# Depthwise convolution of a two-block kernel: seven of 31 taps moved to GpSimd, one from TensorE to VectorE's share, a modulation pair placed behind the taps

## The reference

```
u = h @ w_pw1 + b_pw1            # 1024 -> 2048
a, g = split(u);  v = a * sigmoid(g)
v = dwconv(v, w_dw, b_dw)        # depthwise, 31 taps, pad 15, each channel alone
v = silu(layernorm(v, ln_g, ln_b))
return v @ w_pw2 + b_pw2
```

## Time and profile before

| | |
|---|---|
| median of three runs | 2652.66 us |
| the profiled execution | 2652.95 us |
| its span | 2651.1 us |
| PE busy | 2338.6 us, 88% |
| DVE busy | 1311.8 us, 49% |
| ACT busy | 927.6 us, 35% |
| POOL busy | 732.1 us, 28% |
| L1234, the taps on DVE | 448 instructions, 235.9 us |

### The profile page before, as it was taken

How to read it: one execution, slowest core, us unless ns; L and a number is a source line. 1 busy time by engine, 2 the same in 40 slices (tenths; PEclk the granted TensorE clock), 3 DMA queues, 4 the chain that set the end, 5 groups by cost and what they waited for, 6 DMA issues and landing times.

```text
span 2651.1 us, 35320 instructions
## 1 busy us (share of the span) xinstructions
PE 2338.6 (88%) x13455; PEld 1920.8 (72%) x13455; DVE 1311.8 (49%) x2171; ACT 927.6 (35%) x1388; POOL 732.1 (28%) x344
## 2 busy tenths in 40 slices
PE   3888647999999997999979999989967888999998
PEld 3777436888888886767767787767636887778877
DVE  3599973433123324568553213456665554542441
ACT  4211143543123313455444323434452222442341
POOL 2122102223222221310133434433102222344342
PEclk7999868999999998999989999999887998999999
DMA  7656301122112221200023323332100001233332
GB/s 250 223 192 213 108 7 58 48 64 75 52 56 63 69 59 52 72 25 1 18 87 87 97 86 95 104 104 80 52 0 1 1 1 43 85 90 92 95 96 87
DMA packets 337222, 204.70 MB, mean 77 GB/s; under 512 B 5918, under 2 KB 335304, under 8 KB 336968
## 3 DMA queue, kind: packets, MB, share of 16 engines
q1 hardware_dynamic: 331915, 194.02, 24.4%
q10 hardware_dynamic: 5180, 8.94, 1.0%
HBM read 200.74 MB, written 2.20 MB: 77 GB/s over the span
## 4 chain that ended last, share of the span: by engine, by line
PE 38%; issue 31%; DVE 15%; POOL 10%; ACT 3%; DVEq 1%; DMA 1%; ACTq 0%; POOLq 0%
PE ps L575 10%; POOL w_lo L517 10%; PE ps L576 10%; PE ps L577 10%; DVE ps L1234 9%; PE ps L2449 1%; PE ps L2447 1%; PE ps L2439 1%; PE ps L1500 1%; DVE n_t L960 1%; DVE m L2608 1%; PE ps L776 1%; ACT w_hi L547 0%; DVEq L2629 0%; DMA x_rows<-in_ctx 0%
## 5 line engine op out<-in xcount | busy, mean ns | idle before, releaser
L517 POOL TENSOR_TENSOR w_lo<-raw,w_hi 128x1024 fp32r<-128x1024 f32 (+1 forms) x253 | 645.2, 2552 | 1523.0 <-ACT w_hi L547 1504.4
L575 PE MATMUL ps<-x_hi,w_hi 128*128 128x512 f32 (+1 forms) x1864 | 683.1, 366 | 67.8 <-DVE x_lo L1137 49.4
L576 PE MATMUL ps<-x_lo,w_hi 128*128 128x512 f32 (+1 forms) x1864 | 669.0, 359 | 0.0
L577 PE MATMUL ps<-x_hi,w_lo 128*128 128x512 f32 (+1 forms) x1864 | 667.2, 358 | 0.0
L547 ACT ACTIVATE w_hi<-raw 128x1024 fp32r<-128x1024 f32 (+1 forms) x251 | 280.9, 1120 | 836.7 <-PE ps L577 830.8
L575 PEld LDWEIGHTS ps<-x_hi,w_hi 128*128 128x128 f32 x1864 | 356.6, 191 | 141.1 <-issue 68.5
L576 PEld LDWEIGHTS ps<-x_lo,w_hi 128*128 128x128 f32 x1864 | 357.3, 192 | 53.0 <-issue 3.8
L577 PEld LDWEIGHTS ps<-x_hi,w_lo 128*128 128x128 f32 x1864 | 356.7, 191 | 51.8
L1401 DVE SCALAR_TENSOR_TENSOR f_a<-ps,prm,f_a 128x511 f32<-128x511 f32 (+2 forms) x176 | 116.1, 681 | 375.6 <-ACT f_b L1367 364.7
L575 PE MATMUL ps<-g_hi,w_hi 128*128 128x512 f32 (+1 forms) x704 | 259.5, 369 | 14.7 <-DVE g_lo L1410 10.5
L576 PE MATMUL ps<-g_lo,w_hi 128*128 128x512 f32 (+1 forms) x704 | 257.6, 366 | 0.0
(11 more groups left out here) (346 smaller groups left out, 3017.1 us busy)
## 6 DMA issues: line engine op xcount, KB each, us to landing
raw<-in_ffn_w_up SPq DMA_DIRECT2D x88, 512.0 KB, 3.8
ada_tail<-in_ada_w SPq DMA_DIRECT2D x22, 1024.0 KB, 8.2
raw<-in_ffn_w_down SPq DMA_DIRECT2D x32, 704.0 KB, 4.5
raw<-in_w_up SPq DMA_DIRECT2D x44, 512.0 KB, 3.8
ada_s<-in_ada_w SPq DMA_DIRECT2D x20, 1024.0 KB, 9.0
raw<-in_conv_w_pw SPq DMA_DIRECT2D x24, 512.0 KB, 4.1
raw<-in_w_down SPq DMA_DIRECT2D x16, 704.0 KB, 4.6
raw<-in_w_in SPq DMA_DIRECT2D x17, 512.0 KB, 3.9
```

The source lines that it names most:

```text
L517: pool.tensor_tensor(M.w_lo[:, slot, 0:K * P], M.raw[:, slot, 0:K * P], M.w_hi[:, slot, 0:K * P].bitcast(F32), ALU.subtract).then_inc(lo_r ...
L575: pe.matmul(o, wh, hi[:, k, t0:t0 + tn], start=(k == 0), stop=False)
L576: pe.matmul(o, wh, lo[:, k, t0:t0 + tn], start=False, stop=False)
L577: return pe.matmul(o, wl, hi[:, k, t0:t0 + tn], start=False, stop=(k == K - 1))
```

## The change

TensorE's taps go from three to two (`PE_TAPS`), GpSimd takes seven (`POOL_TAPS`), VectorE has the remaining 22 (28 before). For tile j GpSimd (`taps_pool`) multiplies `vp` with the column of weights into an accumulator `pc` (first tap) or into one of two scratch tiles `pt` (the others: two instructions, 512 and 256 columns), waits for its own product, and adds it to `pc` (768 columns). VectorE adds `pc` to the sum in PSUM behind its last tap, when GpSimd's seven are done. `vp` becomes a ring of three tiles; `pc` and `pt` lie where its other tiles lay. In GpSimd's order the block of tile j - 1 stands behind the `w_lo` of chunks 2j and 2j + 1; the additions to `cv_sum` come one tile later than before. The gating product of the next tile stands in front of VectorE's tap number 13 instead of 18. On TensorE, `taps_pe(j)` comes behind the second modulation pair; the third, where there is one, comes behind `taps_pe(j)`.

```
--- before.py
+++ after.py
@@ -16,7 +16,8 @@
 HD = 64
 TAPS = 31
 PAD = TAPS // 2
-PE_TAPS = 3
+PE_TAPS = 2
+POOL_TAPS = 7
 EPS = 1e-6
 GN_EPS = 64e-5
 L2_EPS = 1e-12
@@ -237,7 +238,9 @@
         self.ada_first = [ada_x[:, i, :, :] for i in range(6)] + [ada_tail[:, i, :, :] for i in range(2)]
         self.ada_ring = [ada_tail[:, i, :, :] for i in range(2)] + [ada_s[:, i, :, :] for i in range(2)]
 
-        self.vp = at("vp", r_g, [KD, self.vw])
+        self.vp = at("vp", r_g, [3, self.vw])
+        self.pc = at("pc", r_g + 4 * self.vw * 4, [2, TOK])
+        self.pt = at("pt", r_g + 4 * self.vw * 4 + 2 * TOK * 4, [2, TOK])
         self.cv = at("cv", r_g + KD * self.vw * 4, [KD, TOK])
 
         o = r_g
@@ -402,6 +405,8 @@
     gate_ready = sem("gate_ready")
     v_ready = sem("v_ready")
     tap_done = sem("tap_done")
+    pool_tap = sem("pool_tap")
+    pool_prod = sem("pool_prod")
     cv_ready = sem("cv_ready")
     cv_cent = sem("cv_cent")
     diag_ready = sem("diag_ready")
@@ -825,7 +830,7 @@
         for tap in range(PE_TAPS):
             for t0, t1, at in ((0, SEQ, VLAT), (SEQ, TOK, VCTX)):
                 mm = pe.matmul(M.pair(j % 2, t0, t1), M.diag[j % 2][tap],
-                               M.vp[:, j, at - PAD + tap:at - PAD + tap + t1 - t0], start=(tap == 0),
+                               M.vp[:, j % 3, at - PAD + tap:at - PAD + tap + t1 - t0], start=(tap == 0),
                                stop=(tap == PE_TAPS - 1))
         mm.then_inc(pe_taps, 1)
 
@@ -837,7 +842,7 @@
             ada_products(pe, M.ada_ring[2 * n % 4:2 * n % 4 + 2], ADA_FIRST + 2 * n)
 
         for j in range(8):
-            first, *others = pairs_of(j)
+            first, second, *third = pairs_of(j)
             if j == 0:
                 first_two(pe, "pw1", BOTH, "n10")
                 ada(first)
@@ -845,9 +850,10 @@
                 products(pe, "pw1", j // 2, 2 * (j % 2), BOTH)
                 ada(first)
                 products(pe, "pw1", j // 2, 2 * (j % 2) + 1, BOTH)
-            for n in others:
+            ada(second)
+            taps_pe(pe, j)
+            for n in third:
                 ada(n)
-            taps_pe(pe, j)
         turn_mods_pe(pe, 1)
 
     def add_mods(dve, lo, hi, n):
@@ -1197,8 +1203,8 @@
 
     VLAT, VCTX = PAD, SEQ + 3 * PAD
 
-    DVE_TAPS = TAPS - PE_TAPS
-    NEXT_AT = 18
+    DVE_TAPS = TAPS - PE_TAPS - POOL_TAPS
+    NEXT_AT = 13
 
     def pw1_dve(dve):
         q0 = Q0["pw1"]
@@ -1208,7 +1214,7 @@
             dve.wait_ge(tile_done, done(q0 + 2 * j + 2))
             dve.wait_ge(gate_ready, done(j + 1))
             for t0, t1, at in ((0, SEQ, VLAT), (SEQ, TOK, VCTX)):
-                ins = dve.scalar_tensor_tensor(out=M.vp[:, j, at:at + t1 - t0], in0=M.pair(j % 2, t0, t1),
+                ins = dve.scalar_tensor_tensor(out=M.vp[:, j % 3, at:at + t1 - t0], in0=M.pair(j % 2, t0, t1),
                                                scalar=M.col("conv_b_pw1", j), in1=M.gate[:, j % 2, t0:t1],
                                                op0=ALU.add, op1=ALU.mult)
             ins.then_inc(v_ready, 1)
@@ -1223,16 +1229,40 @@
             for i in range(DVE_TAPS):
                 if i == NEXT_AT and j < 7:
                     gated(j + 1)
-                tap = PE_TAPS + i
+                tap = PE_TAPS + POOL_TAPS + i
                 for n, (t0, t1, at) in enumerate(((0, SEQ, VLAT), (SEQ, TOK, VCTX))):
-                    src = M.vp[:, j, at - PAD + tap:at - PAD + tap + t1 - t0]
+                    src = M.vp[:, j % 3, at - PAD + tap:at - PAD + tap + t1 - t0]
                     w = M.prm[:, cw + tap * 8 + j:cw + tap * 8 + j + 1]
                     o = M.pair(j % 2, t0, t1)
-                    step = 2 * (DVE_TAPS * j + i) + n
+                    step = (2 * DVE_TAPS + 1) * j + 2 * i + n
                     if i:
                         dve.wait_ge(tap_done, done(step - 1))
                     dve.scalar_tensor_tensor(out=o, in0=src, scalar=w, in1=o, op0=ALU.mult, op1=ALU.add)\
                         .then_inc(tap_done, 1)
+            dve.wait_ge(tap_done, done((2 * DVE_TAPS + 1) * (j + 1) - 1))
+            dve.wait_ge(pool_tap, done(POOL_TAPS * (j + 1)))
+            dve.tensor_tensor(M.pair(j % 2), M.pc[:, j % 2, :], M.pair(j % 2), ALU.add).then_inc(tap_done, 1)
+
+    def taps_pool(pool, j):
+
+        acc = M.pc[:, j % 2, :]
+        pool.wait_ge(v_ready, done(j + 1))
+        if j >= 2:
+            pool.wait_ge(tap_done, done((2 * DVE_TAPS + 1) * (j - 1)))
+        for n in range(POOL_TAPS):
+            tap = PE_TAPS + n
+            c = COL["conv_w_dw"] + tap * 8 + j
+            dst = M.pt[:, n % 2, :] if n else acc
+            for t0, t1, at in ((0, SEQ, VLAT), (SEQ, TOK, VCTX)):
+                ins = pool.tensor_scalar(dst[:, t0:t1], M.vp[:, j % 3, at - PAD + tap:at - PAD + tap + t1 - t0],
+                                         M.prm[:, c:c + 1], zero_col, ALU.mult, ALU.add)
+            ins.then_inc(pool_prod, 1)
+            pool.wait_ge(pool_prod, done(POOL_TAPS * j + n + 1))
+            if n:
+                pool.wait_ge(pool_tap, done(POOL_TAPS * j + n))
+                pool.tensor_tensor(acc, acc, dst, ALU.add).then_inc(pool_tap, 1)
+            else:
+                pool.drain().then_inc(pool_tap, 1)
 
     def pw1_act(act):
         groups = 0
@@ -1257,7 +1287,7 @@
 
     def copy_conv(act, j):
         pair = j % 2
-        act.wait_ge(tap_done, done(2 * DVE_TAPS * (j + 1)))
+        act.wait_ge(tap_done, done((2 * DVE_TAPS + 1) * (j + 1)))
         act.activation(M.cv[:, j, :], M.pair(pair), ACT.Identity, bias=M.col("conv_b_dw", j)).then_inc(cv_ready, 1)
         act.wait_ge(cv_ready, done(j + 1))
         act.drain().then_inc(evac, 2)
@@ -1302,7 +1332,11 @@
         for j in range(8):
             diag_pool(pool, j)
             low_stream(pool, "pw1", 2 * j, 2 * j + 2)
-            cv_sum_pool(pool, j - 2)
+            cv_sum_pool(pool, j - 3)
+            if j:
+                taps_pool(pool, j - 1)
+        cv_sum_pool(pool, 5)
+        taps_pool(pool, 7)
         low_stream(pool, "pw2", 0, 2)
         cv_sum_pool(pool, 6)
         low_stream(pool, "pw2", 2, 8)
@@ -2731,7 +2765,7 @@
 
     @block.gpsimd
     def _(pool):
-        prime(pool, [P_S.sem, lo_ready, zero_ready, diag_ready, cv_sum])
+        prime(pool, [P_S.sem, lo_ready, zero_ready, diag_ready, cv_sum, pool_tap, pool_prod])
         pool.memset(M.p_rows[:, PT - 1, :], 0.0)
         pool.memset(M.one[:, 0:1], EPS)
         pool.memset(M.one[:, 1:2], GN_EPS)
```

18 lines of the change are left out of this document (12 added, 6 removed).

## The result

The changed kernel takes 2635.52 us (median of five runs, 2631.04 to 2639.96) against 2652.86 for the kernel before on the same chip: a ratio of 0.9931, 95% interval 0.9914 to 0.9948, or 17 us less. The prediction said 2660, 7 us more. It had most of the structure of the stage right, the price of one instruction wrong, and the end of the stage wrong.

A forecast was written before the change was run, and what follows sets the result against it. VectorE's chain was taken to bound the first convolution's stage; after the change, 273.75 plus three GpSimd blocks of 25.5 put its end at 350.3 against 343.43, +6.9 us on 2652.95, so 2660, range 2640 to 2679.

The forecast's parts named there:

- the price of GpSimd's TENSOR_SCALAR: GpSimd's taps: a 512- and a 256-column product together taken as 2.0 us, giving a block of 25.5 us.
- it can only push up: GpSimd's taps: two operations and two column operands, unpriced by the trace, could only raise the product's cost; no size given.
- The lowest end, 1.05: GpSimd's taps: cheapest bound for the two products, 1.05 us with a small fixed part, giving a block of 18.9.
- if the block is under 21 us: Sign on GpSimd's block of seven taps: under 21 us, the forecast is wrong and rival 3 holds.
- 273.75 + 3B: VectorE's end of the stage, B being GpSimd's block of seven taps; with 25.5 it gives 350.3 against 343.43.
- A second term: the end: Stage's end: after the last gating product VectorE needs 34.55 us for taps and additions, ending at 350.3.
- Gating 7 comes 36.0 + 1.1 later: Last tile's gating product on VectorE: comes 36.0 + 1.1 us behind the end of GpSimd's block 5.
- The start: Stage's start: VectorE begins near 88.8 instead of 101.15, stops from 102.5 to 116.1, and the head start is lost.
- The cycle: Two tiles of the stage: 41.3 us plus GpSimd's block, 66.8 with 25.5, where they took 60.9 before.
- rival 1: GpSimd's product pair costs like a two-input operation, 2.30 us; GpSimd bounds throughout; +16 us, 2669; chance 0.21.
- rival 3: GpSimd's products have a small fixed part, pair 1.05 us, block 18.9; -13 us, 2640; chance 0.21.
- The shares: Chances given for the whole kernel's outcome: faster 0.27, same 0.27, slower 0.46.

The follow-up runs named there:

- run 3: Changed kernel with GpSimd's two TENSOR_SCALAR forms exchanged: taps as product alone, diagonals as product and sum with a column of zeros; 2675.23 us.
- run 1: Changed kernel with the third modulation pair put back ahead of TensorE's taps; 2648.84 us, the mean's subtraction at 337.76 us.
- run 5: Changed kernel with the load queue reordered, two modulation pairs ahead of the two weight chunks; 2620.85 us, ratio 0.9888 to the kernel before.
- run 2: Changed kernel with the third modulation pair moved behind the next tile's first product; 2627.64 us, ratio 0.9894 to the kernel before.

## Why the prediction was wrong

**The failed step: the price of GpSimd's TENSOR_SCALAR.** "Its slope is not in the trace", and then a bound from one row at 128 columns plus a slope between 0.84 and 2.13 ns: 1.64 to 2.30 us a pair, 2.0 taken. The pair cost 1.31. The slope of 0.83 was the lower one; but the row itself was of another form, and "the new form has two operations and two column operands in place of one ...; it can only push up" is the sentence that run 3 contradicts. At 128 columns the new form takes 442 ns for the old one's 600. The lowest end, 1.05, which I kept for the range, was nearer than the value that I took, and the sign "if the block is under 21 us" came true (20.7). By the prediction's own sum, 273.75 + 3B, the right block of 20.7 gives 335.9 for VectorE's end in place of 350.3: 14.4 us of the error, and the sign. The Trainium skill, GPSIMD Engine Reference, section Engine selection, has one-input operations at about line rate. By the 1.2 GHz of the same page's section Specifications, one column a cycle is, as an estimate, 0.83 ns. The form with two operations agrees (0.83 measured); for the form with one run 3 shows 2.5, three times as much, and the measurement decides.

**A second term: the end.** VectorE ended at 326.6, not 335.9. I let the third pair of tile 6 wait for w_lo like those of tiles 2 and 4 ("Gating 7 comes 36.0 + 1.1 later"). But `w(i)` returns at once for i >= 16, so in that turn no weight load stands ahead of the modulation loads. The profile shows the pair used at 269.76, directly behind the taps (266.99 + 2.85), and no stop before gating 7:

```profile
269.76 1.96 PE L781 MATMUL ps<-ada_s,sc 128*32 128x128 f32 x64
```

Block 5 ended at 266.82 and gating 7 at 292.0, 25.2 us later, where the sum had 37.1: 11.9 us. Block 5 itself ended 2.6 later than the sum has it with a block of 20.7 (264.2), which leaves 9.3. That `w(i)` returns at once was to be read from the code.

**What held.** The start: gating 1 at 116.42 (116.1 said), VectorE at 88.45 (88.8), the head start lost. The cycle, made of the w_lo behind the block and the load behind the w_lo: 41.3 + 20.7 = 62.0, measured 63.85 from the end of block 1 to that of block 3 (141.13 to 204.98) and 61.84 from there to that of block 5. The good fit of the second is luck in part: its load was there 9.6 us behind w_lo, not the 11.2 of the sum, and its third pair took 3.46 us at half the clock, not 1.95; in the first they were 11.5 and 3.64. Run 1 lengthens the cycle by what is put behind the pair, and run 5, which removes the dependence, takes 17.5 us off. The slower regime of rival 1: 371.0 against 369.3 in run 3. VectorE's 1.05 a tap and 0.96 for the addition, in every run. So rival 3 (a cheap pair, 2640) came nearest, with its reason half right: the fixed part fell to 0.34, not to 0.2. That its time came near is luck too. The block of 20.7 alone gives 335.9 by the sum, 7.5 us less than before and not 13; the rest is the wrong end.

**Slips in the numbers.** The shares as the prediction lists them add up to 0.27 faster, 0.24 the same and 0.49 slower, not 0.27, 0.27 and 0.46. A change of 5.3 us either way is by its sum a block between 21.5 and 25.0, not 21.3 and 24.9.

**Small and unforeseen.** L1305 took 1.56 us at the full clock, where L1275 took 2.94 at half before: 1.4 of the 18.6 us. Why is open (see the last section).

## What to carry to other kernels

Price an instruction by rows of its own form: the operation's name isn't enough, as the form with one operation cost GpSimd three times as much a column as that with two, and the richer form was the cheaper. When work moves to an idle engine that works in order, look at what stands behind it there and follow that through the queues: here it was a load queue waiting for a subtraction, and reordering it was worth almost as much again as the whole change (17.5 us at the mean for 18.6). Check the last turns of a loop apart, since waits that end with the data end there.

## What the runs showed of the hardware

GpSimd's float32 TENSOR_SCALAR with a column operand: product alone 600, 924, 1564 ns at 128, 256, 512 columns; product and sum with a second column 442, 558, 771. Its TENSOR_TENSOR at 768 columns took 1.80 to 1.86 us in the changed kernel, 1.80 at 309.48 while VectorE's taps ran and 1.85 at 103.23 while VectorE stood, and VectorE's taps kept 1.05 us beside GpSimd's: no slowing of either by the other is seen.

TensorE's clock at the stage's end, in windows over the two parts of the mean, first of the changed kernel, then of run 1 (from:to, length, busy us of the engines, clock, load share, GB/s):

```profile
324.15:327.05 2.90, 2.90 (x6) 1.57 (x6) 2.77 (x8) 0.38 (x1) 0.00 (x0) 0.50 0.49 146
327.62:329.18 1.56, 1.55 (x4) 0.68 (x4) 0.11 (x2) 0.00 (x0) 0.00 (x0) 1.00 0.00 0
```

```profile
331.30:334.20 2.90, 2.90 (x6) 1.57 (x6) 2.77 (x8) 0.35 (x1) 0.00 (x0) 0.50 0.50 148
334.80:337.73 2.93, 2.93 (x4) 1.17 (x4) 0.10 (x2) 0.00 (x0) 0.00 (x0) 0.50 0.00 0
```

In both L1301 runs at half the clock (0.50) after 17 us of idling, and L1305 follows 0.57 and 0.60 us behind it: at the full clock, 1.56 us, in the changed kernel, and at half, 2.93 us, in run 1. So two stretches that look the same to a few hundredths of a microsecond got different clocks. With a gap of 1.92 us (run 2) or more it ran at half the clock, with none (runs 3 and 5) almost wholly at the full one. What decides between them is not shown, and a difference of 1.4 us at this place is not to be put down to an edit.
